# Pairing the weight loads of an expert loop: 16-KB pieces in place of 8-KB pieces

## The reference

```
top_v, top_e = lax.top_k(logits, 4)              # 520 tokens, 32 experts, 4 of them per token
gates = softmax(top_v)
for each expert e, for the rows xb of the tokens that chose it:
    hh = xb @ w_up[e] + b_up[e]                  # (rows, 1024) @ (1024, 2048)
    gate = minimum(hh[:, :1024], 7);  lin = clip(hh[:, 1024:], -7, 7)
    y  = (gate * sigmoid(1.702 * gate) * (lin + 1)) @ w_down[e] + b_down[e]   # (rows, 1024) @ (1024, 1024)
out[token] += gates * y
```

## Time and profile before

| what | value |
|---|---|
| median of three runs | 1338.73 us |
| span of the profiled execution | 1337.8 us |
| TensorE matmul busy | 1283.2 us, 96% |
| VectorE busy | 918.0 us, 69% |
| ScalarE, GpSimd busy | 285.1 us, 124.1 us |
| DMA traffic | 468.95 MB, of which 441.56 MB on SP's queue q1 |
| mean granted TensorE clock | 0.995 |

### The profile page before, as it was taken

The page is one execution under the profiler, slowest core; times in us unless marked ns, Lnnn a source line. Parts: engine busy times, 40 slices in busy tenths (PEclk is TensorE's granted clock), DMA queues, the critical chain, the costliest instruction groups (busy, mean ns, idle before and its releaser), DMA issues.

```text
span 1337.8 us, 21359 instructions
## 1 busy us (share of the span) xinstructions
PE 1283.2 (96%) x6323; PEld 520.2 (39%) x6323; DVE 918.0 (69%) x1877; ACT 285.1 (21%) x542; POOL 124.1 (9%) x229
## 2 busy tenths in 40 slices
PE   8999999999999999997999998899999997999996
PEld 6876565553333333332333332233333331333332
DVE  3215357656878777775787786687777875777778
ACT  4331143433112121111121121111121111121114
POOL 2000000000020110100110101010111100110100
PEclk9998999999999999999999999999999999999999
DMA  9405154078999999999999999999999999999996
GB/s 358 129 4 191 32 176 170 32 284 342 417 386 386 421 421 419 416 421 421 420 398 423 414 422 420 414 422 407 420 417 420 414 421 421 421 402 420 412 414 274
DMA packets 91409, 468.95 MB, mean 351 GB/s; under 512 B 11870, under 2 KB 29520, under 8 KB 41074
## 3 DMA queue, kind: packets, MB, share of 16 engines
q1 hardware_dynamic: 75070, 441.56, 81.2%
q0 software_dynamic: 7360, 16.79, 3.2%
q10 hardware_dynamic: 8948, 10.19, 2.2%
HBM read 614.82 MB, written 28.77 MB: 481 GB/s over the span
## 4 chain that ended last, share of the span: by engine, by line
PE 71%; DMA 21%; DVE 4%; SPq 2%; issue 1%; ACT 0%; DVEq 0%; POOL 0%; POOLq 0%; ACTq 0%
PE ps L2159 34%; DMA raw<-in_w_down_dram 19%; PE ps L2284 17%; PE ps L1845 5%; PE ps L1822 5%; PE ps L2060 3%; SPq L614 1%; DMA raw<-slot_outputs 1%; PE ps L2173 1%; DVE v_gate L1756 1%; DMA x_rows<-expert_inputs,row_idx 1%; PE ps L1924 0%; PE ps L2007 0%; PE ps L2015 0%; PE ps L2014 0%
## 5 line engine op out<-in xcount | busy, mean ns | idle before, releaser
L2159 PE MATMUL ps<-raw,xT 128*64 128x512 f32 x2816 | 617.4, 593 | 17.6 <-DMA raw<-in_w_up_dram 17.0
L1632 DVE STREAM_TRANSPOSE xT<-x_hold 32x192 f32<-32x192 f32 (+2 forms) x680 | 275.0, 404 | 154.1 <-PE ps L2159 133.9
L2159 PEld LDWEIGHTS ps<-raw,xT 128*64 128x64 f32 x2816 | 199.9, 137 | 424.6 <-issue 391.0
L2284 PE MATMUL ps<-raw,aT 128*64 128x512 f32 x1408 | 317.1, 595 | 16.7 <-DMA raw<-in_w_down_dram 16.7
L1632 DVE STREAM_TRANSPOSE aT<-act_g 32x256 f32<-32x256 f32 x352 | 223.5, 635 | 64.4 <-PE ps L2284 54.5
L2284 PEld LDWEIGHTS ps<-raw,aT 128*64 128x64 f32 x1408 | 97.6, 137 | 229.2 <-issue 174.7
L1016 ACT ACTIVATE act_s<-act_g 128x512 f32<-128x512 f32 x46 | 29.0, 630 | 632.6 <-DVE act_g L1616 632.6
L566 POOL DMA_INDIRECT slot_outputs<-y_rows,out_idx x44 | 45.2, 1028 | 609.3 <-ACT y_rows L1021 608.4
L1404 DVE STREAM_TRANSPOSE bias_up<-up_cols 128x1024 f32<-128x1024 f32 x46 | 57.3, 1245 | 1.6
L1845 PE MATMUL ps<-w_c_cols,hT 128*128 128x512 f32 x128 | 56.8, 596 | 0.0
L558 POOL DMA_INDIRECT x_rows<-expert_inputs,row_idx x47 | 49.3, 1049 | 71.2 <-issue 53.5
(11 more groups left out here) (405 smaller groups left out, 899.7 us busy)
## 6 DMA issues: line engine op xcount, KB each, us to landing
raw<-in_w_up_dram SPq DMA_DIRECT2D x356, 1024.0 KB
raw<-in_w_down_dram SPq DMA_DIRECT2D x180, 1024.0 KB, 10.5
slot_outputs<-zeros ACTq DMA_DIRECT2D x1, 8320.0 KB, 27.9
ahead<-in_w_up_dram SPq DMA_DIRECT2D x8, 1024.0 KB
raw<-slot_outputs SPq DMA_DIRECT2D x8, 1024.0 KB, 16.1
w_c_cols<-in_w_in_dram SPq DMA_DIRECT2D x1, 4096.0 KB, 31.1
w_out_sb<-in_w_out_dram SPq DMA_DIRECT2D x1, 4096.0 KB, 13.8
w_a_cols<-in_w_in_dram SPq DMA_DIRECT2D x1, 2624.0 KB, 12.3
```

What stands on the lines that cost most here:

```text
L1632: dve.transpose(dst_at(rows_out, group), src_at(rows_in, parity)).then_inc(done, 1)
L2159: ins = mm(ps[SUB * i:SUB * i + SUB, banks[bank], :], rows_in[:, j, :], weights[:, c:c + HF], start=False, stop=(j == at_end), skip_group_ ...
L2284: ins = mm(ps[SUB * i:SUB * i + SUB, 2, :], aT[:, j, r, :], raw[:, units[j], D * r + HF * i:D * r + HF * i + HF], start=False, stop=(j == ...
```

## The change

In the loop of SP, up units 3 and 4, up units 5 and 6, down units 0 and 1, and down units 2 and 3 are loaded by one DMA instruction for each pair, 2 MiB in size. The two units of a pair have neighbouring places in `raw` (5 and 6; 0 and 1; 3 and 4; 7 and 8), so a pair is 16 KB in one piece for each partition, in DRAM and in SBUF. Up units 0, 1, 2 and 7 are loaded singly as before. SP waits before a pair until both of its old units have been used. The pair raises the semaphore of its first unit when all of it has landed; TensorE waits for that one before the first unit of the pair, and does not wait before the second. The blocks ahead of the loop and the last down weights are loaded as before. The places, the order of the units, the products and the number of bytes are the same.

```
+UP_LOADS = ((0,), (1,), (2,), (3, 4), (5, 6), (7,))
+UP_HEAD = [units[0] for units in UP_LOADS for _ in units]
...
+            def load_up_pair(e, j, cond):
+                src = w_up[0, column(e)].rearrange("a (p c) n -> c p a n", c=UPU)[j:j + 2].rearrange("c p a n -> p (a c) n")
+                sp.sem_inc(weights_asked, 1)
+                sp.dma_start(raw[:, SLOT[j]:SLOT[j] + 2, :], src, cond=cond).then_inc(landed[j], 16)
+
+            def load_down_pair(e, j, cond):
+                src = w_down[0, column(e)].rearrange("a (p c r) n -> p (a c) (r n)", c=DNU, r=2)[:, j:j + 2]
+                sp.sem_inc(weights_asked, 1)
+                sp.dma_start(raw[:, SLOT[UPU + j]:SLOT[UPU + j] + 2, :], src, cond=cond).then_inc(landed[UPU + j], 16)
...
             with sp.Fori(4, nb) as b:
                 e_up, new_up = expert(sp, b), is_new(sp, b)
-                for j in range(UPU):
-                    sp.wait_ge(up_used, UPU * b + (j + 1 - UPU))
-                    load_up(e_up, j, new_up)
-                load_downs(b)
+                for units in UP_LOADS:
+                    sp.wait_ge(up_used, UPU * b + (units[-1] + 1 - UPU))
+                    if len(units) == 2:
+                        load_up_pair(e_up, units[0], new_up)
+                    else:
+                        load_up(e_up, units[0], new_up)
+                e_dn, new_dn = expert(sp, b - 1), is_new(sp, b - 1)
+                for j in range(0, DNU, 2):
+                    sp.wait_ge(dn_used, DNU * b + (j + 2))
+                    load_down_pair(e_dn, j, new_dn)
...
                 for j in range(UPU):
-                    pe.wait_ge(landed[j], 16 * b + 16)
+                    at = j if isinstance(b, int) else UP_HEAD[j]
+                    if at == j:
+                        pe.wait_ge(landed[at], 16 * b + 16)
                     up_products(j, xT, (0, 1))
...
-                        pe.wait_ge(landed[UPU + j], 32 if isinstance(b, int) and b == 0 else 16 * b + 16)
+                        if isinstance(b, int):
+                            pe.wait_ge(landed[UPU + j], 32 if b == 0 else 16 * b + 16)
+                        elif j % 2 == 0:
+                            pe.wait_ge(landed[UPU + j], 16 * b + 16)
```

## The result

The changed kernel takes 1359.67 us in the median (1356.01 to 1361.19, four runs), against 1338.73 before (four runs too): a ratio of 1.0147 [1.0128, 1.0165], so some 20 us slower. The forecast was 1342, with a range that ended at 1350.

A forecast was written before the change was run, and what follows sets the result against it. The loop was taken as bound by DMA transfers. Terms 1.6 - 10.1 + 12.8 - 1.3 + 0.5 = +3.5 us on the 1337.8 us span gave 1341.3, plus 0.9 for the median: 1342; 80% range 1332 to 1350.

The forecast's parts named there:

- Packets, places, issues: In the loop: 16700 packets fewer, unchanged places, next down pair issued 0.83 us before down units 2+3 land.
- twelve fronts: Ends of down products where TensorE and DMA both meet; the forecast counted twelve and charged its gap at each.
- (a): Once, at 407 us: the pair waits for its second unit's issue at 409.30 with no queued cover, +1.6 us.
- (b): At every front: the later pair issue leaves DMA still for 1.07 us (0.3 to 1.6), +12.8 us over twelve.
- (c): At four fronts where DMA's share was already below 1.01: standing still already there is deducted, -1.3 us.
- The packet saving: On the DMA queue: 116 pairs each save 9 packets at 9.7 ns, 87 ns a pair, -10.1 us.
- (d): At each front TensorE finishes one unit later after the landing, 3.66 instead of 1.94 us; +0.5 us in all.
- Rival 1: At the fronts: the gap does not open; about -6 us, 1333, or 1329 if all is saved; chance 0.20.
- Rival 4: In the pair loads: pieces are not 16 KB, only completion packets are saved; +12.5 us, 1351; chance 0.05.
- Rival 2: On the DMA queue: a packet's fixed cost is small, 5.3 ns, pairs save 5.5 us; +8.1, 1347; chance 0.17.
- Rival 3: At each front: the pair frees its places 1.72 us later, TensorE arrives late; 0.9 us more each, 1353; chance 0.10.
- The chances: For the whole kernel: faster by over 0.3% 0.20, same 0.36, slower 0.44.

The follow-up runs named there:

- 0+1 alone: The changed kernel with down units 2 and 3 single again, up pairs kept: 1353.15 us, ratio 1.0096 to the kernel before.
- both edits and 8-KB pieces: Against the kernel before: loads stay single with 8-KB pieces, but are asked for and awaited in twos; 1361.65 us, ratio 1.0173.

## Why the prediction was wrong

By its own steps:

- **Packets, places, issues: right.** 16704 packets fewer for 16700; the issue at 0.85 us before the front for 0.83; one wait of 1.21 us before unit 2 (539.24), for the announced 1.2 to 1.5 (the two waits that it replaces are 0.55 us each in the earlier trace rows, not 0.94); dips around twelve fronts and, besides 407, nowhere else in the loop. That twelve fronts count is right, though there are fifteen.
- **(a), right.** From 406 to 412 us the changed kernel moves 2 x (221 + 8 + 164) = 786 KB of 2526, 4.1 us too few; the kernel before moves 1672, 2.0 too few. +2.1 for the forecast +1.6. The first front came only 0.45 us later, since the pairs ahead of it had saved time.
- **(b), the step that failed.** The gap was worked out as 1.07 us (0.3 to 1.6) from one constant of 1.9 us for start and receipt, with full rate up to the moment the queue is empty and from the moment it starts again. Measured: the period of three blocks grew by 1.75 us net of what eight pairs saved, 0.4 to 0.7 us (at 55 or 85 ns each), which makes 2.2 to 2.4 us a front; by the packet records, in which idle engines and slow packets take 2.85 us in the mean of the twelve fronts and 0.73 before the change, it is 2.1. Either is above the upper bound. The constant was too low: a pair that finds the queue dry needs 1.9 to 2.6 us from its issue to its last completion packet beside 4.88 of data, and TensorE goes on some 0.5 us behind that, 2.4 to 3.1 in all. Both of the other assumptions were wrong too. The rate falls before the queue is empty, since the engines of a pair end 1.2 to 2.8 us apart (1.13 us of mean idle time), and the first packets of the restart take twice their time (0.60 us). Eleven periods times 1.05 to 1.35 us are 12 to 15 us of the 18 that were missing.
- **(c), mis-sized.** The four shares give 4 x (0.14 + 0.11 + 0.04 + 0.01) = 1.2 us, not 1.3, and the GB/s of the same rows give 2.5. Nor does it come back: at 690 to 694 the kernel before moves 324 GB/s, and by the packet records no front of the twelve loses less than 2.3 us after the change, where before it none lost more than 1.7.
- **The packet saving, right where it can be seen.** -10.1 us stood in the sum, 87 ns a pair. The period of a fresh expert, which loses nothing, shows 85 (31.10 for 30.76, four pairs), and the announced 30.8 came true. Over three blocks the up pairs alone show 55, and 69 by the median. The packet records give the parts: 309 ns for 8 KB and 611 for 16, 7 ns saved by joining two, and 9 ns for a completion packet of 4 bytes, 8 x 7 + 9 = 65 ns a pair; the rest isn't in the packets' own times. That 9.7 ns from two rounded equations came so near is in part luck: the other pair of queues gave 5.3. If the 55 to 69 ns held for all pairs, 2 to 4 us would be missing here.
- **(d), right in place and wrong in size.** One unit's lateness was given 0.5 us in all. Behind the last front alone stand 2.65 us, of which 1.7 are the second unit (3.65 for 1.94). The kernel that only awaits units in twos shows what (d) overlooked: by holding the first unit it also holds the next issue, 18 us in all.
- **The rivals.** Rival 1, no gap, is refuted by the rows of the twelve fronts; what holds there is true only at the three with up units in the queue. Rival 4 is refuted by the packet count. Rival 2, a packet cost of 5.3 ns or 48 ns a pair, is below the 85 ns of the fresh periods and near the 55 of the others; its 1347 too is low by the gap. Rival 3 named what happens, the pair as one grain that frees its places later, but priced it as TensorE's lateness; it is DMA's. Its 1353 was the nearest.
- **The chances.** Slower had 0.44, the most of the three, but the sum rested on two large terms that nearly cancel, -10.1 and +12.8, each from a constant that no row showed alone. The first held and the second didn't. The bounds were set on the constants and not on the model between them.

The Trainium skill ("DMA: Bandwidth & Descriptors", section "Anatomy of one DMA — SWDGE (gpsimd) path") puts a fixed cost of about 2.0 us on a transfer, most of it the receipt. For a pair on a dry queue the trace has 2.4 to 3.1 us beside the data from issue to TensorE's start, somewhat more, and that section is on the other path of issue. Most of it isn't receipt here: 1.0 us passes before the first packet starts (0.96 to 1.00), and some 0.5 us between the last completion packet and TensorE's start. The same page, section "Bandwidth", has the rule to batch to 1 MiB or more for 75% of the peak. In this loop the kernel with 1-MiB loads moves 417 GB/s from 467 to 1270 us, and those with two and three pairs of 2 MiB for an expert, where they cost little, 418 and 420: past that size there was little to win, and the rule says nothing of what a larger grain costs where its place is freed late.

## What to carry to other kernels

Where each buffer exists once, the size of a load is also the grain in which places come free: read, at each point where consumer and transfers meet, how much work is still queued when the next load is asked for, and join only loads that have several microseconds in front (here 3.2 us and more cost little, 2.0 to 2.7 cost about 1 us a time, and eight up units in front hid it whole). Price a gap from a row of that queue running dry, with GB/s beside the busy share, up to the return of full rate, and not from a constant. And where the forecast is a small rest of two large terms, its range must hold an error of each.

## What the runs showed of the hardware

- A queue that restarts isn't at rate at once: 246, 246 and 393 GB/s in the first three microseconds, at busy shares of 1.19, 0.61 and 0.92, and first packets of 0.66 to 1.62 us for 0.61. The first packet starts 0.96 to 1.00 us after the issue.
- The 16 engines end one load at different times: 1.2 to 2.8 us apart for the last down pair of eleven fronts of the changed kernel, 3 us for a down unit before it.
- Engines can be busy and slow: 311 GB/s at a share of 0.94.
- TensorE's clock fell to 1.2 GHz for 3.4 or 6.8 us in or right behind single waits of 1.9 to 4.4 us (1.97 with 0+1 alone, 2.39 with both edits and 8-KB pieces, 3.72 in the changed kernel, 4.10 in the one with two up pairs), but not at each of them: with down pairs alone it stood three waits of 2.96 us. A fall in a down product at a front lengthened the product from 7.09 to 8.78 us. The kernel before, with waits of 1.3 us at most in its loop, keeps its full clock there.
